# A Fourier mixer's token transform moved from every chunk to the normalised rows, and its channel transform merged over groups

## The reference, cut to what matters

```python
D_MODEL, SEQ, C_WIDTH, C_GROUPS, C_GROUP_DIM = 2048, 256, 4096, 16, 256

def fourier_mixer(h, w_in, w_out):
    b, l, _ = h.shape
    u, gate = jnp.split(h @ w_in, 2, axis=-1)
    ug = u.reshape(b, l, C_GROUPS, C_GROUP_DIM).astype(jnp.float32)
    f = jnp.fft.fft2(ug, axes=(1, 3), norm="ortho").real.astype(h.dtype)
    y = f.reshape(b, l, C_WIDTH) * jax.nn.silu(gate)
    return y @ w_out

# in the layer: h = layer_norm(x) * (1 + scale) + shift; x = layer_norm(ALPHA * x + g * out) * gain + bias
```

## Time and profile before

| | |
|---|---|
| median of 3 runs | 2486.27 us |
| the profiled execution, its span (the only time the profile gives of it) | 2488.6 us |
| TensorE matmuls busy | 2419.9 us, 97% |
| VectorE, ScalarE, GpSimd busy | 1652.7, 1045.3, 221.9 us |
| matmuls of first and second transform, busy | 28.9 and 39.0 us |
| HBM read | 584.85 MB, 236 GB/s over the span |

### The profile page before, as it was taken

How to read it: one execution, slowest core, us unless ns; L and a number is a source line. 1 busy time by engine, 2 the same in 40 slices (tenths; PEclk the granted TensorE clock), 3 DMA queues, 4 the chain that set the end, 5 groups by cost and what they waited for, 6 DMA issues and landing times.

```text
span 2488.6 us, 38209 instructions
## 1 busy us (share of the span) xinstructions
PE 2419.9 (97%) x15588; PEld 2073.0 (83%) x15588; DVE 1652.7 (66%) x1869; ACT 1045.3 (42%) x1386; POOL 221.9 (9%) x200
## 2 busy tenths in 40 slices
PE   5999999999999999999999999999999999999996
PEld 1688776579888899888998888888889999999995
DVE  8655654456888888886678566555665485765557
ACT  2454863224333333333343454444543433334432
POOL 0139800011000000000010100000002000000000
PEclk8999999999999999999999999999999999999998
DMA  9844489958999999998554754334446585766461
GB/s 387 338 158 153 153 297 391 388 201 300 356 357 349 371 363 351 351 348 295 161 186 143 235 158 130 104 104 136 165 140 214 184 296 162 242 222 189 151 191 55
DMA packets 257583, 589.46 MB, mean 237 GB/s; under 512 B 20608, under 2 KB 29824, under 8 KB 256128
## 3 DMA queue, kind: packets, MB, share of 16 engines
q1 hardware_dynamic: 257408, 587.02, 68.1%
HBM read 584.85 MB, written 2.10 MB: 236 GB/s over the span
## 4 chain that ended last, share of the span: by engine, by line
PE 90%; DVE 4%; DMA 2%; ACT 2%; issue 1%; POOL 1%; SPq 0%; DVEq 0%; ACTq 0%
PE psum L213 13%; PE psum L225 13%; PE psum L227 12%; PE psum L226 12%; PE psum L215 12%; PE psum L214 12%; PE psum L297 3%; DMA start_slots<-in_w_ada 2%; PE psum L2569 1%; PE psum L1918 1%; DVE wlo L202 1%; PE psum L755 1%; PE psum L535 1%; PE psum L1932 1%; PE psum L882 1%
## 5 line engine op out<-in xcount | busy, mean ns | idle before, releaser
L202 DVE TENSOR_TENSOR wlo<-raw,whi 128x1024 fp32r<-128x1024 f32 (+2 forms) x728 | 881.2, 1226 | 537.7 <-ACT whi L196 534.1
L196 ACT CAST whi<-raw 128x1024 fp32r<-128x1024 f32 (+2 forms) x728 | 738.3, 1022 | 923.9 <-PE psum L227 485.5
L225 PE MATMUL psum<-hh,whi 128*128 128x256 f32 x2688 | 757.4, 282 | 1.3 <-POOL hl L512 0.8
L227 PE MATMUL psum<-hl,whi 128*128 128x256 f32 x2688 | 748.5, 278 | 0.0
L226 PE MATMUL psum<-hh,wlo 128*128 128x256 f32 x2688 | 748.5, 278 | 0.0
L225 PEld LDWEIGHTS psum<-hh,whi 128*128 128x128 f32 x2688 | 505.2, 188 | 17.8 <-DVE wlo L202 11.7
L227 PEld LDWEIGHTS psum<-hl,whi 128*128 128x128 f32 x2688 | 509.2, 189 | 0.0
L226 PEld LDWEIGHTS psum<-hh,wlo 128*128 128x128 f32 x2688 | 505.0, 188 | 1.9 <-issue 1.0
L213 PE MATMUL psum<-whi,hh 128*128 128x512 f32 (+1 forms) x720 | 290.0, 403 | 2.7 <-POOL hl L512 1.4
L215 PE MATMUL psum<-whi,hl 128*128 128x512 f32 (+1 forms) x720 | 280.5, 390 | 0.0
L214 PE MATMUL psum<-wlo,hh 128*128 128x512 f32 (+1 forms) x720 | 278.9, 387 | 0.0
(11 more groups left out here) (396 smaller groups left out, 2463.3 us busy)
## 6 DMA issues: line engine op xcount, KB each, us to landing
araw<-in_ada_w SPq DMA_DIRECT2D x128, 512.0 KB, 6.4
raw<-in_w_in_fourier SPq DMA_DIRECT2D x128, 512.0 KB, 3.9
raw<-in_w_ffn_gate SPq DMA_DIRECT2D x88, 512.0 KB, 8.8
raw<-in_w_ffn_up SPq DMA_DIRECT2D x88, 512.0 KB, 7.7
raw<-in_w_ffn_down SPq DMA_DIRECT2D x88, 512.0 KB, 9.3
raw<-in_w_in_attn SPq DMA_DIRECT2D x88, 512.0 KB, 4.2
araw<-in_w_ada SPq DMA_DIRECT2D x80, 512.0 KB, 6.7
start_slots<-in_w_ada SPq DMA_DIRECT2D x64, 512.0 KB, 8.2
```

The lines of the kernel that those rows point to most:

```text
L196: nc.scalar.copy(whi[:, u % SPLITS, 0:kn, 0:w], raw[:, u % RING, 0:kn, 0:w]).then_inc(s_hi, 1)
L202: nc.vector.tensor_tensor(wlo[:, u % SPLITS, 0:kn, 0:w], raw[:, u % RING, 0:kn, 0:w], whi[:, u % SPLITS, 0:kn, 0:w].bitcast(F32), ALU.subt ...
L225: nc.tensor.matmul(o, h, hh[:, kt + k], start=(kt + k == 0 and f % 2 == 0), stop=False)
L227: ins = nc.tensor.matmul(o, h, hl[:, kt + k], start=False, stop=(kt + k == KT - 1 and f % 2 == 1))
```

## The change: what it does, and the diff

- In chunk 0, behind units 4 to 11, TensorE transforms the normalised rows over the tokens: eight rounds of four plain fp32 matmuls (`token_dft_pe`). The 256 result columns hold 129 cosine and 127 sine frequencies. VectorE applies scale and, in column 0 alone, the shift (`token_dft_dve`); ScalarE and GpSimd split the result into `hfh` and `hfl`, which the up units use in place of `hh` and `hl`.
- The first transform per chunk, ScalarE's four copies and the second transform are gone. One transform over channels (`channel_dft_pe`) takes their place, eight plain fp32 matmuls over both groups at once (129 or 127 columns of each), with the table as the stationary operand. It stands behind unit 3 of the next chunk (unit 4 in chunk 1, and in the last chunk also behind unit 20).
- Buffers move. The channel tables lie in the second half of `araw`, so the sums in chunks 2 and 4 use two slots in place of four. Gain, bias and gate row of the last layer lie over `hh` and `hl`; gain and bias are loaded within the last eight weight loads.
- The gate row is made in chunk 7 in place of 6. `ada_reduce` moves from behind unit 19 to behind unit 17, and `ada_store` from behind the chunk to step 20.

```diff
+    def ada_slot(q, kt):
+        g = pair_rank(q)
+        if g < 8:
+            return kt % 4, SLOT_USES[1] + 4 * g + kt // 4 + 1
+        return kt % 2, SLOT_USES[1] + 32 + 8 * (g - 8) + kt // 2 + 1
     def ada_load(sp, q, kt):
...
         else:
-            sp.wait_ge(s_acc, n - 3)
+            sp.wait_ge(s_acc, n - 3 if g < 8 else n - 1)
...
     def hidden_up_dve(dve, H, c):
         if H.fourier:
-            if later:
-                dve.wait_ge(H.f1, c)
-                dve.wait_ge(H.a, c)
+            dve.wait_ge(s_mm, H.used(c, 15))
+            if c >= 1:
+                dve.wait_ge(H.f, c)
             nc.vector.tensor_copy(ub[:], psum[:, 2:4]).then_inc(H.ub, 1)
...
+    def token_dft_pe(pe, r):
+        n = 40 + r
+        if r == 0:
+            pe.wait_ge(s_dft, 32)
+        pe.wait_ge(s_h32, n - 1)
+        for j in range(2):
+            kt = 2 * r + j
+            for t in range(TT):
+                ins = nc.tensor.matmul(psum[:, 4 + r % 2, j * S:(j + 1) * S], xn[:, t, kt * P:(kt + 1) * P], dft[:, t],
+                                       start=(t == 0), stop=(t == TT - 1))
+        ins.then_inc(s_tp, 1)
+    def token_dft_dve(dve, r):
+        n = 40 + r
+        dve.wait_ge(s_tp, n + 1)
+        dve.wait_ge(s_hl, n - 1)
+        for j in range(2):
+            kt = 2 * r + j
+            v = psum[:, 4 + r % 2, j * S:(j + 1) * S]
+            nc.vector.tensor_scalar(h32[:, r % 2, j, 0:1], v[:, 0:1], mscale[:, kt:kt + 1], mscalex[:, kt:kt + 1],
+                                    ALU.mult, ALU.add)
+            ins = nc.vector.tensor_scalar(h32[:, r % 2, j, 1:S], v[:, 1:S], mscale[:, kt:kt + 1], None, ALU.mult)
+        ins.then_inc(s_h32, 1)
...
-    def hidden_dft1_pe(pe, H, c):
...
-    def hidden_dft2_pe(pe, H, c):
...
+    def channel_dft_pe(pe, H, c):
         pe.wait_ge(H.ub, c + 1)
+        if c == 0:
+            pe.wait_ge(s_dft, 64)
+        ubv = ub[:].rearrange("p g (k s) -> p k g s", k=2)
+        if c == FCH - 1:
+            pe.wait_ge(s_growc, 16)
+        for half in range(2):
+            for q, fs in enumerate((slice(0, 129), slice(129, 256))):
+                if q == 0:
+                    o = psum[:, 2 + half].rearrange("p (g s) -> p g s", g=2)[:, :, fs]
+                else:
+                    o = psum[:, 6 + half, S:2 * S].rearrange("p (g s) -> p g s", g=2)[:, :, 1:128]
+                for k in range(2):
+                    ins = nc.tensor.matmul(o, tabf[:, q, k, half * P:(half + 1) * P], ubv[:, k, :, fs],
+                                           start=(k == 0), stop=(k == 1))
+        ins.then_inc(H.f, 1)
...
+            if H.fourier and first and j >= 8:
+                pe.wait_ge(s_hl, 40 + j - 7)
             if j < 16:
-                multiply_turned(pe, H.unit(c, j)["u"], 2 * (j % 8), 2 * (j // 8))
+                multiply_turned(pe, H.unit(c, j)["u"], 2 * (j % 8), 2 * (j // 8),
+                                (hfh, hfl) if H.fourier and j >= 8 else None)
...
+                if H.fourier and first and 4 <= j < 12:
+                    token_dft_pe(pe, j - 4)
...
-                if H.fourier and c == 1 and j == 1:
-                    hidden_dft1_pe(pe, H, 0)
                 if H.fourier and j == (4 if c == 1 else 3):
-                    hidden_dft2_pe(pe, H, c - 1)
-                if H.fourier and j == 19:
-                    hidden_dft1_pe(pe, H, c)
-                if H.fourier and c == FCH - 1 and j == 21:
-                    hidden_dft2_pe(pe, H, c)
+                    if c in (3, 5):
+                        pe.wait_ge(s_mod, c // 2)
+                    channel_dft_pe(pe, H, c - 1)
+                if H.fourier and c == FCH - 1 and j == 20:
+                    channel_dft_pe(pe, H, c)
```

## The result

| | before | after |
|---|---|---|
| median of the runs on one chip | 2486.03 us (8 runs) | 2493.47 us (8 runs, 2490.35 to 2494.91) |
| ratio to before, 95% interval | | 1.0025 [1.0016, 1.0034] |
| profiled execution: span | 2488.6 us | 2490.2 us (its time 2491.97) |
| Fourier stage in the traces, start of its first unit to end of the last matmul | 591.6 us | 596.7 us |

The kernel became slower by 7.4 us. The forecast was 2485.0 and the range ended at 2493. The two spans differ by only 1.6 us because the profiled execution of before lost some 4 us far ahead of the change, at 395 to 409 us, in the first block's stage; its granted clock was 0.77 on average there (390 to 412 us), against 1.00 in the profile after. The Fourier stage alone shows +5.2 us in the traces; the other 2 us of the medians are not placed.

A forecast was written before the change was run, and what follows sets the result against it. The prediction took TensorE's own instruction time as the bound. Its terms, -28.7 + 0 + 13.8 + 10.6 + 3.0 = -1.3 us, took 2486.3 to 2485.0 us, range 2475 to 2493.

The forecast's parts named there:

- rival A: The forecast: long gate and up units throughout the Fourier stage; 2485.0 us, own range 2482 to 2489; chance 0.48.
- Second transform removed: TensorE, Fourier stage: eight second transforms of 3.59 us each leave the path, -28.7 us.
- Channel for first transform: TensorE, each chunk: eight matmuls of 258 and 254 columns cost the same 3.45 us as the first transform, 0.
- Token transform: TensorE, chunk 0: eight added rounds behind units 4 to 11, 1.72 us each, all on the path, +13.8 us.
- VectorE, ScalarE and GpSimd in chunk 0: Their added scaling, cast and subtraction per token round just keep pace with TensorE's 4.55 us per unit, 0.
- Long units: TensorE, chunks 0 to 7: 96 units go from 2.72 to 2.83 us behind the wide fp32 transform, +10.6 us.
- the ada slots: Chunks 2 and 4: two slots instead of four delay ada and weight loads in SP's queue, +3.0 us (0 to 7).
- L: Time from a weight load's issue to its landing in chunks 2 and 4; taken as 6.5 us, binding from 5.
- the prediction's own formula: Chunks 2 and 4: TensorE's wait is 7.3 + 3P + 3.1 + L - 34.2, 1.5 us per chunk.
- P: Chunks 2 and 4: time per pair of ada sums through the weight loads, (6.05 + L)/2.
- rival C: Slots decide via SP's queue in chunks 2 and 4: L 8.3 us, wait 6 us per chunk, 2494.0 us; chance 0.13.
- the signs given for A (1 to 4) and for C (6 and more): Chunks 2 and 4: us per chunk of TensorE idle before units 10 to 16, with ScalarE waiting for weight DMAs.

The follow-up runs named there:

- e2: Changed kernel with three slots for the ada sums of chunks 2 and 4 instead of two: 2481.28 us.
- e5: Changed kernel with three ada slots and the channel transform done per group (16 matmuls of 129 and 127 columns): 2474.20 us.
- e10: Changed kernel with three ada slots and token rounds in halves of 128 columns, channel transform still merged: 2479.81 us.
- e8: Changed kernel with two ada slots, each pair of ada loads two weight loads later in SP's order: 2487.19 us.
- e3: Kernel before, with only two slots for the ada sums of chunks 2 and 4, nothing else: 2500.69 us.
- e4: Changed kernel with its two ada slots, channel transform done per group (16 matmuls of 129 and 127 columns): 2486.22 us.
- e6: Changed kernel with three slots, channel transform per group and ahead of unit 0 from chunk 2 on, token rounds in 128-column halves: 2472.53 us.
- e7: Changed kernel with three ada slots, only the second half of the channel transform done per group (12 matmuls): 2472.84 us.
- e9: Changed kernel with four slots, second half of the channel transform per group, the block ahead of unit 0 from chunk 2 on: 2469.91 us.
- e11: Changed kernel with four slots, token rounds in 128-column halves, second half of the channel transform per group: 2473.13 us.

## Why the prediction was wrong

**The forecast path, long units throughout (rival A), is what happened, and the sum without the slots was right.** It said -4.3 us; e2, the change with a third slot, in whose trace TensorE doesn't wait in chunks 2 and 4, shows -5.3 us (ratio 0.9978, that is -7.7 to -3.2). Term by term:

- *Second transform removed, -28.7:* nothing contradicts it. The chunk's period is 70.5 us, as forecast (2091.64 to the next block at 2162.1), down from 72.8.
- *Channel for first transform, 0:* 3.45 us against 3.45. Right.
- *Token transform, +13.8:* its part beyond a long unit is 1.73 us per round. Right.
- *VectorE, ScalarE and GpSimd in chunk 0, 0:* no unit waits there. The 255-column scaling took 0.47 us instead of 0.54, the one-column one 0.27 instead of 0.16. Right.
- *Long units, +10.6:* seen long, but for about a dozen (those behind the waits of chunks 2 and 4, and unit 15 of chunk 7). e5 gives 5 to 7 back with the block alone, e10 1.5 with the token rounds, about 8 of the 10.6. Right in the main.

**The step that failed is the ada slots, "+3.0 us (0 to 7)".** In the trace they cost 5.0 us in chunk 2 and 5.3 in chunk 4, 10.3 in all; by the medians 12.2 (e2), beyond the end of that term. The place was right (waits ahead of units 10 to 16, ScalarE waiting for weights). Three things in its working were not:

- *L, taken as 6.5 us.* Weight loads took 7.9 us in this stretch (DMA issues of after, 2020 to 2060, median us to landing in the last column), ada tiles 5.2:

```profile
raw<-in_w_in_fourier SPq DMA_DIRECT2D x9, 512.0 KB, 7.9
araw<-in_ada_w SPq DMA_DIRECT2D x8, 512.0 KB, 5.2
raw<-in_w_out_fourier SPq DMA_DIRECT2D x8, 512.0 KB, 9.2
```

  The text argued that at most four transfers could be outstanding, "fewer than in the rows with 7.3", and went below those rows. But when loads are released by a wait they leave in a burst: one ada tile and two weights within a microsecond, with the tile before still on its way. The nearest row, with 7.3, should have been the floor of L, where the range of the term ended with it. With 7.9 the prediction's own formula gives P = 7.0 and a wait of 5.0 us per chunk, what chunk 2 shows; that it comes out so close is in part luck, since the formula follows one loop of two.
- *The other loop.* The sum followed the chain through the weight loads, (6.05 + L)/2, and left out the slot's own: landing 6.3 + sum 1.28 = 7.6 us for a pair of tiles with two slots, against TensorE's 5.66. That needed no guess about the queue: the earlier trace rows gives landings up to 7.1 us and 1.33 per sum, so more than 5.66 for every landing above 4.3 us. In e8, where fewer weights stand behind the wait, about half of the loss stays.
- *The clock.* The sum had no term for it. Of the 5.3 us in chunk 4, 1.6 are a unit at a granted clock of 0.50 behind a wait; e3 shows one such stretch behind a wait and e4 two; no other trace, e8 with its waits of up to 2 us among them, shows one in this stage.

So **rival C came nearest** (2494.0 us, from P = 7.2; the sums came 7.2 us apart on average), at a chance of 0.13. Its condition, L = 8.3, was a little higher than the 7.9 of the rows, and its 6 us of waiting a chunk was more than the 5.0 and 5.3 seen, which lie between the signs given for A (1 to 4) and for C (6 and more). Like the forecast it follows the weight loads alone and knows neither the slots' own loop nor the clock, so that its time lies within 0.6 us of the measured one is in part luck. That the kernel is slower by more than 0.2% has 0.16 in the forecast; the interval of the ratio, 1.0016 to 1.0034, leans to that side.

The fit of the Trainium skill, DMA: Bandwidth & Descriptors, section "Anatomy of one DMA", gives as an estimate 3.2 us for 512 KB, but the Trainium skill gives it there for transfers that GpSimd issues, which the prediction left out; these loads are issued by SP. By that estimate no slot would have bound. The rows show 3.7 in a quiet chunk and 7.9 here, and e3 measures 14 us from the slots. The rule of the Trainium skill to issue early and wait late (DMA: Bandwidth & Descriptors, section "Rules for kernel authors") is what e2 bears out: the same loads, one tile further ahead, cost nothing. The Trainium skill, TensorE: Matmul & The Clock Gate, section "Back-to-back issue gap", gives one gap for a width, about 109 ns at 256 columns for a single matmul by itself; the rows show 113 and 118 ns within one kernel at the same granted clock, and e5 that the difference is worth 5 to 7 us.

## What to carry to other kernels

When a change takes buffers from a stream, work out the loop of one buffer first: landing under the traffic of that stretch plus the time until it is consumed, divided by the number of buffers, against the consumer's pace; 7.6/2 = 3.8 us a tile failed here where 7.6/3 = 2.5 sufficed, against 2.83. (At 2.72 us a unit three slots sufficed in e5 and seem just short in e6, so leave a margin.) A load that waits in a queue shared with others costs those too, and once it waits its landing time is that of a burst, so take the loaded rows as the lower bound. And a repeated short sequence whose length differs between places at full clock is a term of its own: here 0.11 us on some 96 units, 10.6 us by the forecast, takes back most of the 14.9 that moving the transform saves by the same forecast.

## What the runs showed of the hardware

- The same 24 fp32r matmuls of 256 columns take 2.72 or 2.83 us at a granted clock of 1.00. Behind blocks of plain fp32 matmuls of 254 to 258 columns they are long, whether those ahead were long (after, e2) or short (e10, and the first transform of before in chunk 1). Blocks that end in narrow ones (127 columns) bring the short length where the units ahead were long (e4, e5, e7, e9), and the long one where they were short (e6, e11). One matmul of 512 columns did either (chunk 7 of after).
- In the kernel before and in the change, units are long at a chunk's beginning, behind the down units of 512 columns; e9 shows 24 of them short once narrow fp32 matmuls stand between.
- The length can change behind a wait, with no other matmul between: in chunk 2 of the change the unit at 2035.03, just behind one, takes 2.84 us with 0.22 for its first matmul, and from there a matmul comes every 0.113 us, where it was 0.118 ahead of the wait. In e6 it changes from 2.72 to 2.83 at 2044.68 with no wait there that the trace shows.
- A record of a plain fp32 matmul of 256 columns costs about 0.215 us beside units, one of 129 or 127 columns about 0.109. With two records each, that is 0.43 and 0.22 us a matmul, so halving the columns and doubling the count costs nearly nothing (3.27 against 3.49 us for the block).
- TensorE's granted clock fell to 0.50 inside the unit that followed an idle time of 2.65 us (chunk 4 of after), for 3.2 us, and 256-column matmuls then came every 0.21 us in place of 0.12; behind 3.01 us in chunk 2 it stayed at 1.00.
